# Attention scores of a two-block hybrid layer stack as three-pass products of half-array heads, begun four steps ahead

## The reference

```python
h = rms_norm(x, norm_g); proj = h @ w_in       # a_q a_k a_v a_g b_q b_k b_v b_g m_q m_g
qa, ka = rope(rms_norm(heads(a_q))), rope(rms_norm(heads(a_k)))   # 6 heads of 64, causal ("moba" at 512 tokens)
qb, kb = rope(rms_norm(heads(b_q))), rope(rms_norm(heads(b_k)))   # 6 heads, causal with counts ("dilated")
qm, km = rms_norm(heads(m_q)), rms_norm(heads(m_k))               # 4 heads, 256 memory rows
o = softmax(q @ k.T * 64**-0.5 + mask) @ v                        # for each of the 16 heads
x = x + concat([oa * silu(a_g), ob * silu(b_g), om * silu(m_g)]) @ w_out
```

## Time and profile before

| | |
|---|---|
| median of 3 runs (lowest, highest) | 1702.03 us (1699.03, 1704.1) |
| the profiled execution, its span | 1697.58 us, 1695.8 us |
| granted TensorE clock, mean | 0.995 |
| TensorE matmuls / weight loads busy | 1619.6 us (96%) / 1321.2 us (78%) |
| VectorE / ScalarE / GpSimd busy | 1010.1 / 729.2 / 57.8 us |
| DMA | 136.23 MB, mean 80 GB/s |

### The profile page before, as it was taken

One profiled execution on the slowest core, in us unless ns is written; L12 is line 12 of the kernel. 1 busy time (PEld: TensorE's weight loads), 2 busy tenths in 40 slices (PEclk: granted clock), 3 DMA queues, 4 the chain that ended last, 5 costly groups with the idle time before them and its releaser, 6 DMA issues.

```text
span 1695.8 us, 21496 instructions
## 1 busy us (share of the span) xinstructions
PE 1619.6 (96%) x8009; PEld 1321.2 (78%) x8009; DVE 1010.1 (60%) x2246; ACT 729.2 (43%) x1503; POOL 57.8 (3%) x80
## 2 busy tenths in 40 slices
PE   6999999999999999999999999999989999997999
PEld 6878777787777878777787877898767779985667
DVE  4597656444444397757443344576886564778663
ACT  4444443333234443543332424434456553344662
POOL 0000002000001000002000001000000010000000
PEclk9999999999999999999999999999999999999999
DMA  7332121332323332112233323332112233211121
GB/s 219 96 87 75 39 61 53 97 98 90 98 89 89 92 92 87 51 50 63 75 96 91 100 87 112 94 84 68 61 33 68 81 87 99 81 49 45 38 75 62
DMA packets 80883, 136.23 MB, mean 80 GB/s; under 512 B 8190, under 2 KB 33420, under 8 KB 80780
## 3 DMA queue, kind: packets, MB, share of 16 engines
q1 hardware_dynamic: 77264, 129.48, 25.5%
q10 hardware_dynamic: 3516, 5.37, 1.1%
HBM read 132.74 MB, written 2.10 MB: 80 GB/s over the span
## 4 chain that ended last, share of the span: by engine, by line
PE 45%; DVE 13%; ACT 4%; issue 2%; POOL 0%; ACTq 0%; DVEq 0%
PE gemm_bank L695 34%; PE aux_bank L762 3%; PE aux_bank L791 3%; DVE w_lo L1340 2%; PE aux_bank L779 2%; DVE rope L1439 1%; ACT w_hi L1021 1%; DVE head_sums L1392 1%; DVE probs L1495 1%; ACT probs L1068 1%; DVE kT L1479 1%; PE aux_bank L750 1%; DVE probs L1507 1%; DVE product L1758 0%; ACT L1293 0%
## 5 line engine op out<-in xcount | busy, mean ns | idle before, releaser
L1021 ACT ACTIVATE w_hi<-raw 128x512 fp32r<-128x512 f32 (+3 forms) x524 | 305.5, 587 | 681.5 <-PE gemm_bank L695 680.1
L1340 DVE TENSOR_TENSOR w_lo<-raw,w_hi 128x512 fp32r<-128x512 f32 (+3 forms) x524 | 330.7, 636 | 445.0 <-ACT w_hi L1021 443.3
L695 PE MATMUL gemm_bank<-act_hi,w_hi 128*128 128x512 f32 x768 | 318.4, 415 | 14.9 <-DVE product L1758 3.8
L695 PE MATMUL gemm_bank<-act_hi,w_lo 128*128 128x512 f32 x768 | 300.8, 392 | 0.0
L695 PE MATMUL gemm_bank<-act_lo,w_hi 128*128 128x512 f32 x768 | 300.2, 391 | 0.0
L695 PE MATMUL gemm_bank<-w_hi,act_hi 128*128 128x384 f32 (+3 forms) x736 | 269.1, 366 | 6.5 <-DVE bq L1380 2.9
L695 PE MATMUL gemm_bank<-w_hi,act_lo 128*128 128x384 f32 (+3 forms) x736 | 257.4, 350 | 0.0
L695 PE MATMUL gemm_bank<-w_lo,act_hi 128*128 128x384 f32 (+3 forms) x736 | 257.4, 350 | 0.0
L695 PEld LDWEIGHTS gemm_bank<-act_hi,w_hi 128*128 128x128 f32 x768 | 144.6, 188 | 57.1 <-issue 12.7
L695 PEld LDWEIGHTS gemm_bank<-act_lo,w_hi 128*128 128x128 f32 x768 | 144.9, 189 | 31.1 <-issue 2.9
L695 PEld LDWEIGHTS gemm_bank<-act_hi,w_lo 128*128 128x128 f32 x768 | 144.5, 188 | 31.1
(11 more groups left out here) (289 smaller groups left out, 2133.7 us busy)
## 6 DMA issues: line engine op xcount, KB each, us to landing
raw<-in_w_in SPq DMA_DIRECT2D x104, 512.0 KB, 3.6
raw<-in_w_in SPq DMA_DIRECT2D x64, 384.0 KB, 3.3
raw<-in_w_out SPq DMA_DIRECT2D x32, 512.0 KB, 3.7
raw<-in_w_branch SPq DMA_DIRECT2D x24, 512.0 KB, 3.8
raw<-in_w_mem_kv SPq DMA_DIRECT2D x8, 512.0 KB, 3.7
raw<-in_w_in SPq DMA_DIRECT2D x16, 256.0 KB, 2.7
raw<-in_w_in SPq DMA_DIRECT2D x8, 416.0 KB, 4.9
x<-in_x SPq DMA_DIRECT2D x4, 512.0 KB, 5.2
```

The source lines that it names most:

```text
L695: last = pe.matmul(o, a, c, start=begin and n == 0, stop=end and n == 2)
L1021: act.activation(w_hi[:, s % RING, 0:n], raw[:, p % RAW, kk % PIECE, 0:n], ACT.Copy)\
L1340: dve.tensor_tensor(w_lo[:, s % RING, 0:n], raw[:, p % RAW, kk % PIECE, 0:n], w_hi[:, s % RING, 0:n].bitcast(F32), ALU.subtract).then_inc( ...
```

## The change

- In block 2 the score product of a unit is three `fp32r` passes, hi\*hi, lo\*hi, hi\*lo, instead of one float32 product. Each head uses its own 64 rows of the array; the two heads alternate. The padded `kT_2`, its memset and the wait for it go.
- ScalarE writes the high parts of the turned q and k (`turned_hi`), after its `w_hi` of the step; VectorE subtracts the low parts (`turned`), for block 2 at the end of the turn's step, after `w_lo` and `extra(n)`. Only these low parts free the banks.
- Scores are begun four steps ahead of their scaling instead of two, if the probabilities' buffer is free by then (four buffers instead of three). Units 0 and 1 of a causal pair, and units 0 and 1, 2 and 3 of a memory pair, share one call and one bank per head.
- In the lead, scores of units 0 and 1 stand together at `bk`'s fifth k-step.

```diff
-                if mine[0] >= 2:
-                    self.begin[mine[0] - 2].append(("scores", m))
+                if mine[0] >= 2 and self.together(m):
+                    last = max(self.together(m)) - self.buffers
+                    free = self.steps_of[last][-1] + 1 if last >= 0 else 0
+                    self.begin[max(mine[0] - SCORES_LEAD[block], free, 0)].append(("scores", m))
+        def together(self, m):
+            if self.block == 1:
+                return {m: 0}
+            kind, i = self.kind(m), m % NT
+            if kind.name == "memory":
+                return {} if i % 2 else {m: 0, m + 1: kind.n_keys(i) * P}
+            return {0: {m: 0, m + 1: P}, 1: {}}.get(i, {m: 0})
...
+        def scores_2(a, m):                                          # TensorE
+            g, kind = m // NT, a.kind(m)
+            if m % NT == 0:
+                aux_wait_read(pe, a.key("q", g, 0))
+                aux_wait_read(pe, a.key("k", g, 0))
+            banks = [aux_open(a.key("S", m, x), S_BANKS[x]) for x in range(2)]
+            for mm, c in a.together(m).items():
+                i, keys = mm % NT, kind.n_keys(mm % NT) * P
+                for n, (qq, kk) in enumerate(((q_hi, k_hi), (q_lo, k_hi), (q_hi, k_lo))):
+                    for x in range(2):
+                        r = slice(x * HD, (x + 1) * HD)
+                        last = pe.matmul(banks[x][:, c:c + keys], qq[r, g % 2, i * P:(i + 1) * P],
+                                         kk[r, g % 2, 0:keys], start=n == 0, stop=n == 2)
...
+        def turned_hi(a, g):                                         # ScalarE
+            for what, hi in (("q", q_hi), ("k", k_hi)):
+                bank = aux_wait_full(act, a.key(what, g, 0))
+                n = T if what == "q" else a.pairs[g][0].k_tiles * P
+                act.activation(hi[:, g % 2, 0:n], bank[:, 0:n], ACT.Copy).then_inc(turned_hi_ready, 1)
...
+            for n, (what, hi, lo) in enumerate((("q", q_hi, q_lo), ("k", k_hi, k_lo))):   # VectorE, turned
+                key = a.key(what, g, 0)
+                columns = T if what == "q" else a.pairs[g][0].k_tiles * P
+                dve.wait_ge(turned_hi_ready, 2 * a.turn_count(g) - 1 + n)
+                dve.tensor_tensor(lo[:, g % 2, 0:columns], aux_bank[aux_place[key][0]][:, 0:columns],
+                                  hi[:, g % 2, 0:columns].bitcast(F32), ALU.subtract).then_inc(read_of(key), 1)
...
             for n, (m, _, _) in enumerate(a.steps):                  # VectorE, attention
+                turns = [event for event in a.begin[n] if event[0] == "turn" and a.block == 2]
                 for event in a.begin[n] + a.middle.get(n, []):
-                    if drain and event[0] == "turn":
+                    if event in turns:
                         drain(event[1])
-                    begin(a, *event)
+                    else:
+                        begin(a, *event)
                 split_beside(split, a, n, evict_beside)
                 extra(n)
+                for event in turns:
+                    begin(a, *event)
```

More of the change, by code:

```diff
@@ L570, in head, with turn_count @@
             return 2 * self.pairs[g][1] + x
+        def turn_count(self, g):
+            return self.l * len(self.pairs) + self.turns.index(g) + 1
         def qT_of(self, g, x):
-            kind = self.pairs[g][0]
-            return qT[self.where][0:kind.rows, g % 2 if kind.group == 2 else (2 * g + x) % 3, :]
+            return qT_1[0:QK, (2 * g + x) % 3, :]
         def kT_of(self, g, x):
-            kind = self.pairs[g][0]
-            return kT_2[:, g % 2, x, :] if kind.group == 2 else kT_1[0:kind.rows, (2 * g + x) % 3, :]
+            return kT_1[0:QK, (2 * g + x) % 3, :]
         def probsT_of(self, g, x, j):
@@ L631, in attention_2 @@
                    DEPTH * UNITS_1 + l * UNITS_2, fill, lambda n: 1.3 if n < 13 else 0.9)
-        a.lead = {4: [("turn", 0, 0)], 5: [("scores", 0)], 6: [("scores", 1)]}
+        a.lead = {4: [("turn", 0, 0)], 5: [("scores", 0)]}
         for g, (at_pair, step) in {1: (0, 1), 2: (0, 3), 3: (2, 1), 4: (2, 3), 5: (3, 3), 6: (4, 3), 7: (5, 3)}.items():
             a.turn_at(g, 0, a.first_step_of(at_pair) + step)
+        a.turns = list(range(len(a.pairs)))
         return a
@@ L763, in scores @@
                           a.kT_of(g, x)[:, 0:n_keys * P], start=True, stop=True).then_inc(full_of(key), 1)
+        def scores_2(a, m):
[11 more added lines that the diff above has]
+                                         kk[r, g % 2, 0:keys], start=n == 0, stop=n == 2)
+                        if n == 2 and mm == max(a.together(m)):
+                            last.then_inc(full_of(a.key("S", m, x)), 1)
         def begin(a, what, *of):
@@ L778, in turn_probs @@
                     c = (x * (j1 - j0) + j - j0) * P
[L779 removed]
+                    last = pe.transpose(bank[:, c:c + P], probs[a.where][m % a.buffers][:, x, j * P:(j + 1) * P], ident[:, :])
             last.then_inc(full_of(key), 1)
@@ L1059, in evict_now, with exponential @@
                 act.activation(dst(b), gemm_bank[b][:, 0:groups[gi].n], func).then_inc(gemm_read[b], 1)
-        def exponentials(a, m):
[L1062 to L1069, removed]
+        def turned_hi(a, g):
[3 more added lines that the diff above has]
+                act.activation(hi[:, g % 2, 0:n], bank[:, 0:n], ACT.Copy).then_inc(turned_hi_ready, 1)
+        def exponentials(a, m):
+            for mm in a.together(m):
+                for x in range(2):
+                    aux_wait_read(act, a.key("S", m, x))
+                    exponential(a, mm, x)
+        def exponential(a, m, x):
+            keys = a.kind(m).n_keys(m % NT) * P
+            c = a.column(m) + x
+            rows = probs[a.where][m % a.buffers][:, x, 0:keys]
+            act.activation(rows, rows, ACT.Exp, bias=neg_max[:, c:c + 1], scale=-1.0,
+                           accum_out=row_sum[:, c:c + 1]).then_inc(probs_ready, 1)
         def attention(a, evict_beside, extra):
@@ L1077, in attention @@
                         exponentials(a, event[1])
+                    elif event[0] == "turn" and a.block == 2:
+                        turned_hi(a, event[1])
                 bank = aux_wait_full(act, a.key("T", n))
@@ L1472, in turned @@
         def turned(a, g, x):
[L1473 to L1483, removed]
+            if a.block == 1:
+                bank = aux_wait_full(dve, a.key("q", g, x))
+                dve.tensor_copy(a.qT_of(g, x), bank[0:QK, :]).then_inc(read_of(a.key("q", g, x)), 1)
+                bank = aux_wait_full(dve, a.key("k", g, x))
+                dve.tensor_copy(a.kT_of(g, x), bank[0:QK, :]).then_inc(read_of(a.key("k", g, x)), 1)
+                return
@@ L1505, in scaled @@
             for x in range(2):
-                rows = probs[a.where][m % 3][:, x, 0:keys]
+                rows = probs[a.where][m % a.buffers][:, x, 0:keys]
                 ins = dve.tensor_scalar(rows, rows, row_inv[:, c + x:c + x + 1], None, ALU.mult)
```

45 lines of the change are left out of this document (26 added, 19 removed).

## The result

The changed kernel takes 1734.85 us (median of 4 runs, 1733.67 to 1736.69) against 1700.53 us (4 runs of the kernel before on the same chip, 1697.97 to 1704.1): ratio 1.0201, 95% interval 1.0179 to 1.0224. It is slower by 34 us, where the sum forecast 12.6 (1702.03 to 1714.6). The profiled execution took 1733.67 us with a span of 1731.9, against 1697.58 and 1695.8 before: +36.1.

What follows compares the result with a forecast made beforehand. TensorE, busy 1619.6 of 1695.8 us, was taken to bound the kernel. Per layer, 11.8 us saved against 12.2 idling, 0.8 swallowed saving and 5.1 clock gave +6.3, twice +12.6: 1702.03 to 1714 us, range 1690 to 1730.

Steps and rivals of the forecast that it cites:

- the sum: Whole kernel: -11.8 + 12.2 + 0.8 + 5.1 = +6.3 us per layer, twice +12.6; forecast at 50%.
- Score products: TensorE, block 2: three passes take 21.1 us per layer instead of 32.9, saving 11.8.
- the change of shape: TensorE score calls, block 2: switching matmul shape costs 0.3 us per call.
- Heads at once: TensorE score passes: two heads' 64-row products run together; serial-heads rival 14.4 us more per layer, 1743 us, 9%.
- Loads hidden behind matmuls: TensorE score passes: weight loads hide behind matmuls of the same rows; rival that they don't, 1731 us, 5%.
- The late low parts: Block 2, scores after turns: TensorE waits for low parts behind VectorE's other work, 17.4 us per layer.
- What they replace: Block 2: late low parts replace 6.3 us of earlier waits per layer; scaled-probability waits fall from 12.1 to about 6.
- Step 0: Block 2, step 0: the second of two successive score calls waits for bank reads, +1.1 us per layer.
- Sum of the idling: TensorE, block 2: 12.2 us of added idling per layer, from 17.4 against 6.3 and step 0's 1.1.
- Clock: TensorE, block 2: three clock falls per layer after waits, +5.1 us per layer; bounds 0 and 8.5.
- The faster one: Rival, steps after turns: low parts not late, six waits about 1 us each; -10.2 us per layer, 1682 us; 22%.
- The rival without falls: Rival, block 2: the waits stand but the clock doesn't fall; +2.4 us, 1704 us; 14%.

Runs made afterwards that it cites:

- Run 1: Changed kernel with VectorE's low parts of turned q and k moved ahead of the step's `extra(n)`: 1701.54 us, ratio 0.9999 to the kernel before.
- 8, with lead of two: Changed kernel with low parts ahead of `extra(n)` and block 2's scores begun two steps ahead, not four: 1694.78 us, ratio 0.9965 to the kernel before.
- run 10: Changed kernel without low parts: all three passes multiply high parts, ScalarE's copy frees the banks: 1684.37 us, ratio 0.9911 to the kernel before.
- run 11: Changed kernel with 28 unread identity transposes ahead of the score call in five steps per layer: 1713.89 us, ratio 1.0082 to the kernel before.
- run 9: Changed kernel with both heads' products reading rows 0 to 63, the second head's scores left out: 1767.25 us, ratio 1.0393 to the kernel before.
- run 12: Changed kernel, low parts ahead of `extra(n)`, lead of two, seven unread transposes before scores in seven steps per layer: 1694.27 us, ratio 0.9967 to before.
- run 3: Changed kernel with block 2's scores begun two steps ahead instead of four: 1735.07 us, ratio 1.0204 to the kernel before.
- run 6: Changed kernel with score products issued one head after the other, not in turn: 1735.59 us, ratio 1.0216 to the kernel before.
- 4: Changed kernel with the score call of the step after a turn moved behind TensorE's filler products: 1709.79 us, ratio 1.0059 to the kernel before.

## Why the prediction was wrong in size

The direction and the main mechanism held, the range (to 1730) did not. Two steps failed: the clock was priced at three falls per layer, +10.2 us, and its loss grew by 27.3; and the lead of four was given no new waits for scaled probabilities, where it made two per layer, 7.3 us in all. The result can be laid out in columns. Change against the kernel before, in us; the last is what is left for TensorE's work and for all that the other columns miss:

| run | span | waits in block 2 | clock's loss | idle work | rest |
|---|---|---|---|---|---|
| the change | +36.1 | +36.6 | +27.3 | | -27.8 |
| 1, low parts between | +3.8 | +14.1 | +15.4 | | -25.7 |
| 8, with lead of two | -4.7 | +11.6 | +8.5 | | -24.8 |
| 10, no low parts | -13.4 | +7.4 | +1.7 | | -22.5 |
| 11, filled in full | +16.2 | +6.1 | +5.1 | +30.6 | -25.6 |

In these rows the rest is the same within 6 us, and their spans differ by 50. Worked out alike, the other runs (but run 9, whose products cost more) lie between -20.6 (run 12) and -29.6 (run 3), so a single row is good to some 5 us and no better. Part of the spread is clock lost while TensorE waits, which costs nothing (2.7 us in the change).

- **Score products: the paces right, the price of a call too low.** The six products of 512 keys hold 0.90 us (rows of run 6). By the measure of the earlier trace rows, which also counts that the call starts 0.09 us late and that the plain product behind it is followed after 0.33 us and not 0.23, the call costs 1.10 us where I had 0.99. Taken alike at full clock, units 0 and 1 cost 1.10 (1.02 forecast), 384 keys 0.93 (0.82) and a memory call 1.12 (1.02): the change of shape is 0.4 us a call, not 0.3. An estimate from these is 23.3 us per layer instead of 21.1, and 19.2 us saved in both instead of 23.6. The 32.9 us of the kernel before stand (1.73 us for 512 keys, 0.87 for 256, by the same measure). So 3 to 9 us of the rest column are not the products' saving.
- **Heads at once: right**, shown by run 9 (its price is 32.4 us with the clock's share, I had 28.8). Run 6 does not bear on it.
- **Loads hidden behind matmuls: right.** The pass pitches are those that I built from the earlier trace rows. The Trainium skill's rule (TensorE: Matmul & The Clock Gate, Part 3: Packing small matmuls, The mechanism) is that a load overlaps a running matmul only when the row group differs; the same section also has loads into the background weight buffer pulled ahead. The trace disagrees with the "only": in run 9 all products of a call are in one row group, and one of 256 columns takes 0.12 us, hardly over its columns at 2.4 GHz (0.107), so that no time for a load is seen in it.
- **The late low parts: right.** Layer 0's waits were 3.43, 3.22, 3.06, 4.57, 3.60 and 0.59 us where I had 3.5, 3.2, 3.1, 3.9, 3.0 and 0.7; in two layers 36.9 us against 34.8. Runs 1, 4 and 10 go round them in three different ways and take back 33, 25 and 50 us, so they make the slowdown.
- **What they replace: wrong.** I set 6.3 us per layer against them, of which some 3.4 were waits for scaled probabilities that would vanish, and forecast these down to 6 us. They are 12.7. Those at steps 16 and 22 did vanish (1.94 and 1.44 us), and those that I left standing stood: 1.38 us at step 10 (1.84 before), 0.60 at step 13, 0.89 at step 20. But the lead of four made two new ones in each layer: 1.49 us at step 1, behind the two score calls of step 0, and 1.97 at step 34, in a memory pair (1336.60). The failing step was to let the lead touch none of these waits and so to set no term for new ones; under the lead of two neither is there, and run 3 has 5.4 us, my number.
- **Waits that I didn't forecast.** For `mq_flat` and `bgT` 5.6 us more, for `probsT` 3.0 less. The first two are as large in run 10 as in the change and no smaller under the lead of two, so neither the low parts nor the lead make them; what does wasn't tried. Nor was the sharing of a call by two units, or the fourth buffer, varied in any run. Step 0 cost 1.6 and 1.2 us where I had 1.1.
- **Sum of the idling:** 24.4 us forecast, 36.6 measured: the 12.2 between them are 7.2 from the probabilities, 2.1 from the turns, 0.6 from step 0 and 2.3 from the other tiles.
- **Clock: the term that was mis-sized most.** I took three falls per layer at 1.7 us, 10.2 in all, with a bound of 8.5 per layer. There were eight in the first layer and six in the second, and 27.3 us more loss than before. The price of one was right for most (four of the 14 were about 3.4 us, as in the windows at 1288). The count was wrong for two reasons: 11 of the 12 waits of 3 us or more came with one (all six in layer 0, where I took three; in layer 1 the one of 3.22 us did not), and three of the five waits between 1.5 and 2.0 us, which my list left out: for `neg_max` (1.61) and `bgT` (1.71) in layer 0, for probabilities (2.00) in layer 1. The other two, 1.97 in layer 0 and the `bgT` of layer 1 (1.71 again), did not. Two of the 12 are not of the low parts either but for `mq_flat` (3.38). That 1.94 us passed without a fall was a thin reason for leaving the shorter ones out, beside the fall behind 1.9 us of the earlier trace rows.

The two errors, 12.2 us of idling and 17.1 of clock, less 5.8 that the rest column gives back (-27.8 against -23.6 + 1.6 forecast), are the 23.5 us between +12.6 and +36.1. No term of mine stands behind those 5.8 us: the products saved some 4 us less than I took, so that 8.6 us of the change's -27.8 are open, of which 2.7 are the clock lost in waits.

The rivals fared no better. The faster one had waits of about 1 us behind each turn and 1682 us. Run 1 has that condition (14.3 us in 12) and takes 1701.5, as the lead's waits and 18.8 us of lost clock stay; only run 10, with no low parts at all, comes near (1684.4). The rival without falls had 1704; run 11, which fills the waits and keeps most of the clock, takes 1713.9, so that without falls too the idling (12.2 us too small) would have missed it.

## What to carry to other kernels

When a producer's second half is moved to the end of a step, list who waits for the first engine behind it: here two subtractions of 0.68 us behind a wait for squares (in other steps behind norms or gating) cost 33 us, more than the saved products are worth. Look in your own trace which idle gaps of TensorE come with a fall of the clock (here 14 of the 17 of 1.6 us or more), price every gap like them with it and not only the new ones, and test it by filling the gap with work that nobody reads. An order of two edits should be tried in both: the lead of two was worth nothing with the low parts late and 7 us with them early.

## What the runs showed that I had not expected

- Products in different 64-row halves start side by side even when three of one half are issued ahead of the first of the other (run 6: 0.90 us for six products of 512 columns; whether the chip reorders them is not shown); products in the same half don't (run 9: 0.24 us per pair of 256 columns against 0.12).
- Where the gaps are long, the clock's loss passes into the time in full: 21 us of time came back from 22 us of loss with 30.6 us of idle transposes added (run 11). Where they are short it did not: 5.1 us less loss and no time (run 12), which stays open. A transpose of 128 columns that is shown with 0.27 us takes 0.109 in a row.
- Falls come with waits of 1.61 us as well as of 4.57, while waits of 1.97 us (1336.60) and even 3.22 us (1531.39) pass without one: the length of a gap alone does not say.
